# Reordering the work where four attentions begin and end, inside a one-core kernel of two transformer blocks

## What is computed

```python
h_x = rms_norm(x, norm_g) * (1 + sc_x) + sh_x
px, pc = split_cols(h_x @ w_in), split_cols(h_c @ w_in)
oa = mixer_a(...)   # 4 heads of 128, 2 kv heads, rotary; softmax over all 768 keys
ob = mixer_b(...)   # 4 heads, 4 kv heads; a 2-D neighbourhood bias table per head is added to the scores
oc = mixer_c(...)   # 4 heads, 2 kv heads, rotary; window of 128 plus context, with a sink
od = mixer_d(...)   # 4 heads, latent keys and values, all 768 keys
x = x + gt_x * (concatenate([oa, ob, oc, od]) @ w_out)   # each o is softmax(q k + bias) v * silu(g)
```

## Time and profile before

| | |
|---|---|
| runs | 2888.15, 2887.67, 2884.80 us; median 2887.67 us |
| profiled execution | 2882.11 us, span of its trace 2880.3 us |
| TensorE busy | 97% of the span |
| VectorE, ScalarE, GpSimd busy | 37%, 34%, 38% |
| mean granted TensorE clock | 0.991 |
| DMA | 318.31 MB, 111 GB/s on average |

### The profile page before, as it was taken

The page is one execution under the profiler, slowest core; times in us unless marked ns, Lnnn a source line. Parts: engine busy times, 40 slices in busy tenths (PEclk is TensorE's granted clock), DMA queues, the critical chain, the costliest instruction groups (busy, mean ns, idle before and its releaser), DMA issues.

```text
span 2880.3 us, 34712 instructions
## 1 busy us (share of the span) xinstructions
PE 2795.4 (97%) x14062; PEld 2178.5 (76%) x14062; DVE 1062.8 (37%) x1836; ACT 984.7 (34%) x1539; POOL 1093.5 (38%) x541
## 2 busy tenths in 40 slices
PE   7999999999999997999999999999999999999999
PEld 4576888778678874678887778766788888777787
DVE  3244323042331144322203367644223354666311
ACT  4332422242232221432323312455322234666411
POOL 1223123213312330245543344444555455554443
PEclk9999999999999998999999999999999999999999
DMA  9845323212784331424333333322534333223432
GB/s 371 305 128 161 88 74 86 59 43 74 219 159 98 79 83 29 132 60 123 110 96 81 84 92 88 97 79 59 163 115 117 88 89 109 78 74 92 139 114 84
DMA packets 456607, 318.31 MB, mean 111 GB/s; under 512 B 32352, under 2 KB 404960, under 8 KB 455680
## 3 DMA queue, kind: packets, MB, share of 16 engines
q1 hardware_dynamic: 424400, 280.09, 33.5%
q10 hardware_dynamic: 32048, 35.98, 5.0%
HBM read 299.14 MB, written 28.95 MB: 114 GB/s over the span
## 4 chain that ended last, share of the span: by engine, by line
PE 92%; DMA 2%; DVE 2%; ACT 2%; issue 1%; POOL 1%; SPq 1%; ACTq 0%; DVEq 0%; POOLq 0%
PE acc L1914 77%; PE aux L1914 7%; PE ssq L1917 3%; PE ssq L1914 3%; DMA raw<-in_w_in 2%; PE aux L1917 1%; POOL w_lo L1210 1%; DVE rstd L1453 1%; DMA ada_ring<-in_w_ada 0%; ACT w_hi L898 0%; SPq L673 0%; ACT x_t L833 0%; DVE p L1535 0%; ACT p_t L1031 0%; DMA nbr_bias<-nbr_bias_dram 0%
## 5 line engine op out<-in xcount | busy, mean ns | idle before, releaser
L1210 POOL TENSOR_TENSOR w_lo<-raw,w_hi 128x1024 fp32r<-128x1024 f32 x362 | 869.4, 2402 | 1637.5 <-ACT w_hi L898 1637.5
L1914 PE MATMUL acc<-h_hi,w_hi 128*128 128x512 f32 (+1 forms) x3232 | 1203.9, 389 | 9.3 <-POOL w_lo L1210 4.4
L1914 PE MATMUL acc<-h_hi,w_lo 128*128 128x512 f32 (+1 forms) x3232 | 1173.4, 380 | 0.0
L1914 PE MATMUL acc<-h_lo,w_hi 128*128 128x512 f32 (+1 forms) x2464 | 872.7, 376 | 0.0
L898 ACT ACTIVATE w_hi<-raw 128x1024 fp32r<-128x1024 f32 x362 | 383.4, 1059 | 1149.6 <-PE acc L1914 1054.0
L1914 PEld LDWEIGHTS acc<-h_hi,w_hi 128*128 128x128 f32 x3232 | 585.5, 188 | 177.9 <-issue 64.5
L1914 PEld LDWEIGHTS acc<-h_hi,w_lo 128*128 128x128 f32 x3232 | 584.4, 188 | 119.2
L1914 PEld LDWEIGHTS acc<-h_lo,w_hi 128*128 128x128 f32 x2464 | 441.0, 189 | 85.3 <-issue 4.6
L1914 PE MATMUL acc<-out_t_lo,w_hi 128*128 128x512 f32 x768 | 299.0, 389 | 0.0
L1453 DVE RECIPROCAL rstd<-rstd 128x512 f32<-128x512 f32 (+1 forms) x29 | 118.0, 4070 | 350.8 <-ACT rstd L942 350.7
L1914 PEld LDWEIGHTS acc<-out_t_lo,w_hi 128*128 128x128 f32 x768 | 144.4, 188 | 28.7
(11 more groups left out here) (242 smaller groups left out, 2337.4 us busy)
## 6 DMA issues: line engine op xcount, KB each, us to landing
raw<-in_w_in SPq DMA_DIRECT2D x52, 1024.0 KB, 5.9
raw<-in_even_w_in SPq DMA_DIRECT2D x41, 1024.0 KB, 5.6
raw<-in_odd_w_in SPq DMA_DIRECT2D x36, 1024.0 KB, 5.6
ada_ring<-in_w_ada SPq DMA_DIRECT2D x32, 1024.0 KB, 6.9
gate_ring<-in_w_ada SPq DMA_DIRECT2D x16, 1024.0 KB, 7.1
raw<-in_w_out SPq DMA_DIRECT2D x16, 1024.0 KB, 5.9
raw<-in_even_w_out SPq DMA_DIRECT2D x16, 1024.0 KB, 5.8
raw<-in_odd_w_out SPq DMA_DIRECT2D x16, 1024.0 KB, 6.5
```

The lines of the kernel that those rows point to most:

```text
L1210: G_.tensor_tensor(WL[half][:], RAW[G.rs][:, half * HALF * P:(half + 1) * HALF * P], WH[half][:].bitcast(F32), ALU.subtract).then_inc(S["l ...
L1914: return M.matmul(out_, lhsT, rhs, start=start, stop=stop, skip_group_check=True)
```

## The change

It has five parts, all in the first block.

1. **Scores first.** Attend places unit n's scores so that unit 0 falls on the accumulator that the run's last but one group used. TensorE's entry waits only for `xn_done` and `rope_done`, then for the release of that accumulator; scores of unit 1 wait for the release of the other. The waits for `aux_free` and `copied` move to the first product with the values.
2. **Values turned behind them.** If the last group is a value group (a and b), its six turns come between the scores of units 0 and 1, and VectorE's copy to `v_nat` after `maxima(0)`. `flush` no longer does them.
3. **End of attend.** TensorE no longer does `out_turn(15)` nor waits for `out_done`; it goes on with the next run's first group, and does the turn inside it, after k-tile 1.
4. **Bias tables.** ScalarE fetches the tables of heads 0 and 1 behind group 3 of run b, GpSimd adds their mask behind group 7. Their tiles move to addresses that are free by then.
5. **Gate rows.** Rows 2, 3 and 4 are turned behind groups 6, 8 and 10 of run c, into `ssq` columns 960 on; the last row between the scores of units 0 and 1. ScalarE's first exponential in c waits until that row is turned (`p_t` shares its memory). In a, the second row is turned behind group 6 and not 7.

```diff
@@ plan()
+        G.emptied = acc_free[G.c]
...
+            gs[6].fold, gs[8].fold, gs[10].fold = 2, 3, 4
+            gs[2].after_turns = 32
...
-            gs[5].fold, gs[7].fold = 0, 1
+            gs[5].fold, gs[6].fold = 0, 1
...
-            gs[1].chore, gs[9].chore = "load_b", "silu_b"
+            gs[1].chore, gs[3].chore, gs[7].chore, gs[9].chore = "load_b", "bias_in", "bias_add", "silu_b"
@@ build()
-    TB = [at(f"nbr_bias{s}", 14 * GRID_W, 193 * K1 + 3584 * s) for s in range(2)]
+    TB = [at(f"nbr_bias{s}", 14 * GRID_W, (168 + 31 * s) * K1) for s in range(2)]
...
+        slot = lambda item, u: (u + 1 + item["last"][1].cs) % 2
@@ ScalarE
+                elif G.chore == "bias_in":
+                    act.wait_ge(S["nbr_spread"], 16)
+                    act.wait_ge(S["gate_mm"], 8)
+                    nbr(0)
+                    nbr(1)
...
+                    if m == "c" and n == 0:
+                        act.wait_ge(S["bias_turned"], 6)
...
-                if m == "b":
-                    act.wait_ge(S["nbr_spread"], 16)
-                    settled(act, item["total"], ("xn_done", "rope_done", "stage_used", "aux_free"))
-                    nbr(0)
-                    nbr(1)
@@ GpSimd
+                if G.chore == "bias_add":
+                    for h in (0, 1):
+                        add_columns(h)
@@ VectorE, attend
                 maxima(0)
+                side(item["last"][1])
+                gates()
@@ TensorE
+            def fold_row(r):
+                at_, row = (1000 + 8 * r, r) if r < 2 else (960 + 8 * (r - 2), r - 2)
+                pe.wait_ge(S["gate_row"], r + 1)
+                need(pe, "bias_taken", min(r, 2))
+                for j in range(4):
+                    e = mm(SSQ[:, at_ + 2 * j:at_ + 2 * j + 2], GROW[:, 512 * row + j * P:512 * row + (j + 1) * P],
+                           FOLD[:], True, True)
+                e.then_inc(S["bias_turned"], 1)
...
+                            if half == 0 and k8 == 1:
+                                finish_turns()
...
-                settled(pe, item["total"], ("xn_done", "rope_done", "silu_done", "aux_free", "copied"))
-                if m == "c":
-                    pe.wait_ge(S["gate_row"], 6)
-                    for g in range(KT):
-                        e = mm(AUX[:, 640 + 2 * g:642 + 2 * g], GROW[:, g * P:(g + 1) * P], FOLD[:], True, True)
-                    e.then_inc(S["gate_turned"], 1)
-                    pe.wait_ge(S["gate_taken"], 1)
+                last = item["last"]
+                settled(pe, item["total"], ("xn_done", "rope_done"))
...
+                release(pe, last[0].emptied)
                 scores(0)
+                if last[1].kind == "plain":
+                    first(last[1])
+                if m == "c":
+                    fold_row(5)
+                release(pe, last[1].emptied)
                 scores(1)
+                if m == "c":
+                    pe.wait_ge(S["gate_taken"], 1)
...
+                    if n == 0:
+                        settled(pe, item["total"], ("aux_free", "copied"))
...
-                out_turn(15)
-                if m != "d":
-                    pe.wait_ge(S["out_done"], U0 + 16)
+                held.append(out_turn)
```

## The result

The changed kernel took 2862.16 us, median of 4 runs (2859.43 to 2866.27), against 2886.24 us for the kernel before, measured beside it: ratio 0.9925, interval 0.9912 to 0.9937. Two repeats gave 0.9935 (0.9923 to 0.9947) and 0.9926 (0.9911 to 0.9940). The gains of the three medians are 24.1, 15.8 and 22.7 us; the ratios, which are not the quotients of these medians, give 21.6, 18.7 and 21.3. The forecast was 15.3, its first rival 23.0. The median lies outside the forecast's own range (2869 to 2876 us) and inside the range over all cases (2862 to 2878) by 0.16 us only.

The account below looks back on a forecast made before the run. TensorE bounds the kernel, so gains are its idle or low-clock time around attentions: 2.1 + 11.1 + 1.3 + 1.3 - 1.5 + 1.6 - 2.3 + 1.1 + 0.6 = 15.3 us, 2887.67 to 2872.4 us; own range 2869 to 2876, over cases 2862 to 2878.

Parts of the forecast that it names:

- first rival: End of attend c: the rotary load's issue stays at 2.72 us; 23.0 us gained, 2864.7 us; chance 0.25; also called Rival 1.
- the chance for "faster": Whole kernel: faster by more than 0.2% (5.8 us), chance 0.95.
- Starts of a and b: Earlier first turn of `p` in attends a and b: 2.1 us gained in a, 11.1 in b including restored clock.
- Bias work in run b: Table fetches and mask adds moved into run b: hidden in idle time, cost nothing; uncovered 0.7 us.
- Ends of a, b, d: TensorE goes on sooner at the attentions' ends: 1.3 us each at a and b, 0.6 at the late groups.
- the start of d: Scores of attend d begin when the last value matmul ends, without the wait for a copy: 1.1 us gained.
- Rows in run c: Three gate rows turned inside run c, partly covered by waits for `w_lo`: run 1.5 us longer, bounds 0.5 and 2.9.
- Attend c and run d: the step that failed: Rotary load held by the spread, TensorE waits 6.4 us in run d: 1.6 us gained, less 2.3 for low clock.

Follow-up runs that it names:

- experiment 2: Changed kernel with attend b's bias tables fetched and masked at its start again: 2869.24 us, ratio 0.9952 to the kernel before.
- experiment 3: Changed kernel with the last value rows turned and copied before the scores in every attention: 2871.67 us, ratio 0.9960 to the kernel before.
- experiment 5: Changed kernel with three gate rows turned at the start of attend c, not inside run c: 2870.06 us, ratio 0.9948 to the kernel before.
- experiment 7: Changed kernel with the rotary load issued in unit 5 of attend c, behind the undrained spread: 2882.65 us, ratio 0.9994 to the kernel before.
- experiment 4: Changed kernel with the rotary load issued inside run d's first group, not at attend c's end: 2863.43 us, ratio 0.9932 to the kernel before.
- experiment 8: Changed kernel with the 6 MB spread issued at attend c's end, behind store and rotary load: 2893.77 us, ratio 1.0031 to the kernel before.
- third trace of the changed one: Changed kernel unaltered, profiled a third time beside the version with the spread in four pieces: 2861.14 us, ratio 0.9926 to the kernel before.
- experiment 9: Changed kernel with the 6 MB spread issued behind the exponential of attend c's second unit: 2864.60 us, ratio 0.9928 to the kernel before.
- experiment 10: Changed kernel with the spread in four 1.5 MB pieces and the rotary load inside run d, run twice: 2857.29 and 2858.57 us, ratios 0.9912 and 0.9914.

## Why the prediction was right, and where it was not

**The time.** 2862.16 us is in the range over the cases, and the chance for "faster" came true; the forecast of 2872.4 did not. That it came within 10 us owes something to luck: the step below cost the forecast 7 us too much, and a stand that no case held gave part of that back.

**Starts of a and b.** From the run's end to the first turn: 3.64 us in a (costed 3.67), 4.13 in b (4.2). Start of b and what the clock gives back in unit 0, now 3.34 us: 8.9 + 2.3 = 11.2 against 11.1. The row moved up in a, costed at 0.95 in the run, can't be seen under the scatter of what lies ahead; without it the gain at the start of a would be 3.2 us against 3.1. Experiments 2 and 3 show both parts needed.

**Bias work in run b.** Costed at nothing: run b is 188.76 against 188.74 us, and stays there without it.

**Ends of a, b, d.** 1.45 us each at a and b (1.3) and 0.8 at d (0.6). At the start of d the wait of 1 us is gone, as costed; the stage's time can't show it, since it scatters by 2.7 us.

**Rows in run c.** The sum is near (1.4 against 1.5), its reason is not: beside experiment 5 the rows cost 0.2 to 0.3 us, and the rest is a longer wait for `w_lo` that is there without them. The row behind group 6, costed at a full 1.0, covers a wait that a later weight fetch would leave there (experiment 5). Why that fetch lands later, and what lengthens the other waits, stays open.

**Attend c and run d: the step that failed.** "I read 881.78 as a date of the spread, 59.3 us after the run's end, which does not move when the attention gets shorter." The start gave 6.2 us (6.8 costed), and the rotary load's issue moved along with the attention at 2.65 us. The queue does hold a load behind the spread, but until 41.3 us after the spread's issue (experiment 7), long past at the end of attend c; the 2.72 us of the earlier trace rows were mostly the store's doing (experiments 4, 8). TensorE waited 0.81 us and not 6.4, and no low clock followed. Attend c, its ends and run d, costed at 1.6 - 2.3 = -0.7 us together, gave 6.6 in the trace without a stand (c 7.7, run d -1.1), and 2.2 and 0.2 in the two with one. The earlier trace rows show an issue held by the transfers directly ahead of it, and I put it down to the largest one further ahead.

**What no case held.** Rival 1 has the right end of attend c, and its 23.0 us lie near two of the three medians, but above all three ratios. From the kernel before to the third trace of the changed one the stages give a 4.7, b 12.7, run c -1.5, c 7.7, run d -1.1, d 1.0, late -1.2: 22.3 us. In two traces of three attend c is 4.9 and 6.4 us longer, with the stand and the low clock behind it, and in four of twelve a low clock at the end of run c takes 1.6.

The late groups are 1.2 us longer, of which 1.1 arise at one place in the second block, where TensorE waits 4.74 us for a copy and the clock is low (before, then after):

```profile
1855.72 0.77 PE L1914 MATMUL acc<-select_mask,ident_r 128*128 128x256 f32 x2 [4.74 <-DVE q_t L1845]
1854.00:1858.00 4.00, 2.28 (x7) 1.43 (x8) 1.76 (x7) 2.35 (x6) 0.65 (x1) 0.50 0.00 0
1858.00:1862.00 4.00, 4.00 (x16) 2.99 (x15) 3.18 (x7) 1.10 (x4) 2.34 (x2) 0.78 0.00 0
```

```profile
1836.18 0.77 PE L1932 MATMUL acc<-select_mask,ident_r 128*128 128x256 f32 x2 [4.74 <-DVE q_t L1863]
1835.00:1839.00 4.00, 2.82 (x8) 1.84 (x9) 1.80 (x6) 2.35 (x6) 1.19 (x1) 0.60 0.00 0
1839.00:1843.00 4.00, 4.00 (x11) 3.08 (x10) 2.63 (x7) 1.09 (x4) 2.26 (x3) 0.55 0.00 0
```

By these rows and the 0.87 between 1850 and 1854 us before, the low stretch reaches from 1853.0 to 1859.8 us before and from 1835.8 to 1842.6 after, 6.8 us in both. Before, it began 2.8 us ahead of TensorE's restart, after 0.4 us, so 2.3 us more of TensorE's work falls into it and costs 1.2. In all 13 traces of changed kernels it begins 0.4 to 1.3 us ahead of the restart. Why it begins later there stays open; for the kernel before there is one trace.

That the stand is a late code fetch rests on the packet's date in every trace, the stand's place in the program, which never moved, and its absence in all five traces in which the spread was issued behind the packet (experiments 3, 8, 9 and both of 10). That q8 is TensorE's is argued from its size. What decides whether a packet is held 7 us or 20 was not found.

## What to carry over

Ask of a large transfer not only who waits for its data, but what small thing must pass it: here the code of the busiest engine, a weight fetch, and a next issue on the same queue. Here four pieces, each gone in 11 to 12 us, did away with the stand; with the rotary load moved as well this was worth 3 to 4 us by the ratios. When a long issue is seen, look at the transfer directly ahead of it before blaming the largest one, and compare stages over several traces of one kernel before reading a difference of 5 us.

## What the runs showed of the hardware

- TensorE stood for 3.2 to 6.0 us in six traces in which a 16 KB instruction packet ran 19.6 to 22.4 us after a 6 MB spread was issued, and never where it ran before the spread or up to 10.4 us after its issue.
- The issue of one 512 KB load took 2.15 to 3.20 us right behind a 1 MB store, 24.40 us when it came 17 us behind the 6 MB spread, and 0.39 us when it came 6 us behind the store, in one trace with both still undrained. The Trainium skill, "DMA: Bandwidth & Descriptors", section "Issuing engines are not separate DMA queues", calls the sequencer's time for an issue usually small beside the transfer; the 24.40 us are the exception.
- A spread of 6 MB draining beside 1 MB weight fetches stretched the time to landing of three of them from 12.0, 5.7 and 5.8 us to 51.3, 56.9 and 16.3 us.
- A low stretch of the clock of 6.8 us behind the same wait of 4.74 us began 2.8 us ahead of TensorE's restart in one trace and 0.4 to 1.3 us ahead in 13 others, worth up to 1.2 us.
